# Paged attention: two pages side by side on the partitions, interlaced before, in two blocks of 64 after

## The reference, cut to what matters

```
cache_sb_kv  (1, n_pool, 128, 2, 8, 64)   float32: page, token, key or value, head, column
page_table   (8, 64)                      int32

z = q . k / 8 + bias[head]                                  for every past and new token before the query
w = sigmoid(z) * product over later tokens of sigmoid(-z)
out = sum over tokens of w * v
```

## Time and profile before

| what | value |
|---|---|
| median of three runs | 3929.19 us (3927.13 to 3931.07) |
| time of the profiled execution | 3932.51 us |
| its span in the trace | 3930.7 us |
| granted clock of TensorE, mean over the span | 0.958 of full speed |
| busy: TensorE matmul, VectorE, ScalarE, GpSimd | 91%, 48%, 30%, 20% of the span |
| read from HBM | 447.51 MB, of it 512 pages of 512 KB |

### The profile page before, as it was taken

One profiled execution on the slowest core, in us unless ns is written; L12 is line 12 of the kernel. 1 busy time (PEld: TensorE's weight loads), 2 busy tenths in 40 slices (PEclk: granted clock), 3 DMA queues, 4 the chain that ended last, 5 costly groups with the idle time before them and its releaser, 6 DMA issues. The chain is left out here.

```text
span 3930.7 us, 66394 instructions
## 1 busy us (share of the span) xinstructions
PE 3579.0 (91%) x25825; PEld 2949.1 (75%) x25825; DVE 1894.2 (48%) x2770; ACT 1166.0 (30%) x2440; POOL 770.0 (20%) x629
## 2 busy tenths in 40 slices
PE   9988888888777999999998999769987799999998
PEld 9965666666566799999997787446566699999997
DVE  2158574434376634444444366545128934444445
ACT  2156544444412121111114245321115121111112
POOL 0047122222110211111113111036111211111112
PEclk9999999999988999999999999879988899999999
DMA  3110899999703011111112201038523011111112
GB/s 134 45 51 1 337 415 415 413 413 411 307 2 122 12 44 43 43 43 47 49 43 84 70 12 33 20 126 296 172 80 107 24 44 43 43 43 43 43 43 78
DMA packets 187494, 470.75 MB, mean 120 GB/s; under 512 B 31625, under 2 KB 128773, under 8 KB 151382
## 3 DMA queue, kind: packets, MB, share of 16 engines
q1 hardware_dynamic: 166278, 446.50, 30.5%
q10 hardware_dynamic: 20976, 20.97, 1.6%
HBM read 447.51 MB, written 19.91 MB: 119 GB/s over the span
## 5 line engine op out<-in xcount | busy, mean ns | idle before, releaser
L1965 DVE TENSOR_TENSOR x<-x,f_d 128x512 f32<-128x512 f32 x540 | 368.3, 687 | 310.1 <-PE f_d L1777 249.5
L1933 POOL TENSOR_TENSOR f_hl<-f_h,f_hh 128x364 fp32r<-128x364 f32 (+1 forms) x192 | 177.5, 932 | 1267.7 <-ACT f_hh L1893 1267.7
L1982 DVE TENSOR_TENSOR f_h<-f_h 128x364 f32<-128x364 f32 (+1 forms) x192 | 103.1, 537 | 541.3 <-ACT f_h L1887 541.1
L1777 PE MATMUL f_d<-f_w2l,f_hh 128*128 128x512 f32 x896 | 354.4, 396 | 0.0
L1777 PE MATMUL f_d<-f_w2h,f_hl 128*128 128x512 f32 x896 | 354.4, 396 | 0.0
L1777 PE MATMUL f_d<-f_w2h,f_hh 128*128 128x512 f32 x896 | 354.4, 395 | 0.0
L761 DVE COPY ss_kT<-ss_tk 128x512 f32<-128x512 f32 x256 | 176.8, 692 | 327.7 <-PE ss_tk L653 212.0
L1887 ACT ACTIVATE f_h<-f_u 128x364 f32<-128x364 f32 (+1 forms) x192 | 91.2, 475 | 577.4 <-PE f_u L1777 577.4
L1777 PE MATMUL f_u<-xH,w1h 128*128 128x364 f32 (+1 forms) x768 | 254.0, 331 | 2.5 <-DVEq L1967 2.5
L1777 PE MATMUL f_u<-xL,w1h 128*128 128x364 f32 (+1 forms) x768 | 253.8, 330 | 0.0
L1777 PE MATMUL f_u<-xH,w1l 128*128 128x364 f32 (+1 forms) x768 | 253.7, 330 | 0.0
(11 more groups left out here) (588 smaller groups left out, 7893.6 us busy)
## 6 DMA issues: line engine op xcount, KB each, us to landing
ss_kv<-in_cache_sb_kv SPq DMA_DIRECT2D x336, 512.0 KB, 6.4
x<-in_cache_sb_kv SPq DMA_DIRECT2D x176, 512.0 KB, 6.2
w<-in_ffn_w SPq DMA_DIRECT2D x64, 1024.0 KB, 5.2
mp_qb<-mp_q SPq DMA_DIRECT2D x24, 1024.0 KB, 6.7
pe_raw<-in_w_in_even SPq DMA_DIRECT2D x8, 1024.0 KB, 7.1
mp_kc<-in_cache_dil_kv SPq DMA_DIRECT2D x8, 1024.0 KB, 7.7
mp_vc<-in_cache_dil_kv ACTq DMA_DIRECT2D x8, 1024.0 KB, 6.9
mp_w<-in_w_in_odd ACTq DMA_DIRECT2D x7, 1024.0 KB, 6.0
```

The lines of the kernel that those rows point to most:

```text
L1777: mm = pe.matmul(out, a, b, start=(n == 0), stop=(n == len(parts) - 1))
L1933: low = lambda dst, n0, n1, at: g.tensor_tensor(dst, h[:, u % HSLOTS, n0 - at:n1 - at], hh[:, c % 2, f, n0:n1].bitcast(F32), ALU.subtract)
L1965: v.tensor_tensor(K.x[0:r, t, cs], K.x[0:r, t, cs], dn_b[(c * DOWN + u) % 4][0:r, :], ALU.add).then_inc(added, 1)
L1982: v.tensor_tensor(x, x, x, ALU.mult).then_inc(squared, 1)
```

## The change

A page now goes to a block of 64 neighbouring partitions: the first page of a step and sequence to partitions 0 to 63, the second to 64 to 127. Before, the first went to the even and the second to the odd partitions. What runs over the partitions (after the transposes: over the columns) is therefore ordered page first and pair second, and the patterns of the two key copies, of GpSimd's product and of the weights' transposes follow. The number of DMAs, their bytes and their 8,192-byte runs, all instructions and all waits stay as they are, and so does the order of the columns of `kT`, `z` and `left`.

```diff
-                half = self.kv[g % SLOTS][pg::2, 2 * b:2 * b + 2, :]
+                half = self.kv[g % SLOTS][PAIRS * pg:PAIRS * (pg + 1), 2 * b:2 * b + 2, :]
                 sp.dma_start(half, self.cache[bass.ds(page, 1), :, :, :]).then_inc(...)
...
-        w, wT = sb("w", [P, 2, 2, PAIRS, 2]), sb("wT", [P, 2, 2 * PAGE])
+        w, wT = sb("w", [P, 2, 2, 2, PAIRS]), sb("wT", [P, 2, 2 * PAGE])
...
-   mm = pe.transpose(wb[...], w[:, g % 2, r, :, :].rearrange("p q a -> p (q a)"), K.ident[:, :])
+   mm = pe.transpose(wb[...], w[:, g % 2, r, :, :].rearrange("p a q -> p (a q)"), K.ident[:, :])
...
-   v.tensor_copy(kT[:, g % 2, :, j // 2, :, :, j % 2], turn_b[j][...].rearrange("p c (q a) -> p c a q", a=2))
+   v.tensor_copy(kT[:, g % 2, :, j // 2, :, :, j % 2], turn_b[j][...].rearrange("p c (a q) -> p c a q", a=2))
...
-   p.tensor_tensor(w[:, g % 2], z[...].rearrange("p (a q r) -> p r q a", a=2, r=2),
-                   left[...].rearrange("p (a q r) -> p r q a", a=2, r=2), ALU.mult)
+   p.tensor_tensor(w[:, g % 2], z[...].rearrange("p (a q r) -> p r a q", a=2, r=2),
+                   left[...].rearrange("p (a q r) -> p r a q", a=2, r=2), ALU.mult)
```

More of the change, by code:

```diff
@@ L674, in turn_weights @@
                     for r in range(2):
-                        mm = pe.transpose(wb[:, r * P:(r + 1) * P], w[:, g % 2, r, :, :].rearrange("p q a -> p (q a)"), K.ident[:, :])
+                        mm = pe.transpose(wb[:, r * P:(r + 1) * P], w[:, g % 2, r, :, :].rearrange("p a q -> p (a q)"), K.ident[:, :])
                     mm.then_inc(S["w_turned"], 1)
@@ L760, in copy_keys @@
                         v.wait_ge(S["logits"], g - 1)
-                    v.tensor_copy(kT[:, g % 2, :, j // 2, :, :, j % 2], turn_b[j][:, :, :].rearrange("p c (q a) -> p c a q", a=2)).then_inc(k_copied[1], 1)
+                    v.tensor_copy(kT[:, g % 2, :, j // 2, :, :, j % 2], turn_b[j][:, :, :].rearrange("p c (a q) -> p c a q", a=2)).then_inc(k_copied[1], 1)
                 copy_keys(0, 1)
@@ L828, in _ @@
                         p.wait_ge(S["w_turned"], g - 1)
-                    p.tensor_tensor(w[:, g % 2, :, :, :], z[:, g % 2, :].rearrange("p (a q r) -> p r q a", a=2, r=2),
-                                    left[:, g % 3, 1:2 * PAGE + 1].rearrange("p (a q r) -> p r q a", a=2, r=2), ALU.mult).then_inc(S["weights"], 1)
+                    p.tensor_tensor(w[:, g % 2, :, :, :], z[:, g % 2, :].rearrange("p (a q r) -> p r a q", a=2, r=2),
+                                    left[:, g % 3, 1:2 * PAGE + 1].rearrange("p (a q r) -> p r a q", a=2, r=2), ALU.mult).then_inc(S["weights"], 1)
             @block.scalar
@@ L839, in copy_keys @@
                         a.wait_ge(S["logits"], g - 1)
-                    a.activation(kT[:, g % 2, :, j // 2, :, :, j % 2], turn_b[j][:, :, :].rearrange("p c (q a) -> p c a q", a=2), ACT.Copy).then_inc(k_copied[0], 1)
+                    a.activation(kT[:, g % 2, :, j // 2, :, :, j % 2], turn_b[j][:, :, :].rearrange("p c (a q) -> p c a q", a=2), ACT.Copy).then_inc(k_copied[0], 1)
                 def shares(g):
```

## The result

| | before | after |
|---|---|---|
| median | 3929.96 us (4 runs) | 4385.82 us (4362.32 to 4388.68, 4 runs) |
| ratio of the two | | 1.114 (95%: 1.1122 to 1.1159) |
| span of the profiled execution | 3930.7 us | 4386.8 us |
| stage of the change: last matmul of line 689 begins | 1066.8 us | 1517.5 us |

The changed kernel is 11.4% slower. The forecast was 3948 us; the time lies between two of the rivals, "half way" (4117) and "half rate" (4561), and nearer to the latter. The range over all cases (3918 to 4565) holds it; that of the likeliest case (3925 to 3975), on which the forecast stood, doesn't. The instructions of the engines are the same in number and order; what changed is how long the transfers take.

What follows compares the result with a forecast made beforehand. It took page transfers at 413 GB/s to bound one stage, with SP's pace nearly equal. 3932.5 + 2.5 (restart) + 16 (stream) = 3951 us, less 3.3 us to the median: 3948 us, range 3918 to 4565, likeliest case 3925 to 3975.

Steps and rivals of the forecast that it cites:

- half way: Page stream: never leaves its state just after a start, 317 GB/s, +188 us, 4117 us; chance 0.14.
- half rate: Every page of the stage: engines stay on the same half together, 206 GB/s, +623 us, 4561 us; chance 0.30.
- the likeliest case: Transfer-bound stage: both readable collision costs doubled, 3948 us, own range 3925 to 3975; chance 0.40.
- I take it that the engines fall into step as they do now, over a longer way: Page stream: DMA engines recover after each start as before, only later; basis of +2.5 and +16 us.
- the restart: Stage at 430 to 440 us: 320 GB/s against 424 free loses 2.5 us; once more that, +2.5 us.
- the slow stretches after each start: Page stream: collisions that end some 8 us later, three times out of three; taken as evidence against half rate.
- an engine that is one page ahead works on the other half than the one it collided with: Page queue: pages alternate between lower and upper half, so a lead of one page avoids the collision.
- (b): Steady stream: 413 against 424 GB/s costs 16 us as collisions; doubled, +16 us.
- The store: A store running at 206 GB/s against 410, taken as evidence for half rate but weighed below the running stream.
- Can I just issue two DMAs to hit both halves?: Skill section: two concurrent transfers, one to each half, measured only +6% over one; implied half rate for good.
- the marks that I had named: Stage signs: at half rate 206 GB/s, some thirteen slices, TensorE at 4, landing over 20 us, SP waiting nearly every step.

Runs made afterwards that it cites:

- v4: Page stream without attention, each page to the block of partitions 32 to 95: 422 GB/s.
- v7: Page stream without attention, two pages in one DMA on 128 partitions: 422 GB/s.
- e5: The changed kernel with each page on all 128 partitions, one token of 4,096 bytes on each: 3948.25 us, 1.0043 times the kernel before.
- m1: One launch without attention: seven streams of page DMAs from SP into 12 SBUF slots, 96 pages each, differing in destination partitions; 206 to 422 GB/s.
- w1: Page stream of blocks 0 to 63 and 64 to 127 in turn, behind added DMAs of 1, 2, ... 15 runs; its set of four gave 222 to 230 GB/s.
- w4: Page stream of blocks 0 to 63 and 64 to 127 in turn, behind added DMAs of 8 runs; its set of four gave 222 to 230 GB/s.
- u8: Page stream without attention, lower-half pages from SP's queue while upper-half pages come from ScalarE's queue: 239 GB/s together.
- u9: Page stream without attention, upper-half pages from ScalarE's queue while lower-half pages come from SP's queue: 239 GB/s together.
- e6: The kernel before, with SP reading both page numbers of a sequence in one load instead of two: 3930.76 us, 0.9996 times the kernel before.
- v1: Page stream without attention, pages on every second partition: 422 GB/s.
- v3: Page stream without attention, every page to the lower block of 64 partitions: 206 GB/s.
- v2: Page stream without attention, blocks of 64 partitions, lower and upper in turn: 219 GB/s.
- y3: Page stream without attention, two DMAs of 16 rows of 16 KB, step eight from partitions 0 and 4, on eight ports each: between 205 and 241 GB/s.
- w5: Page stream of blocks of 64, lower and upper in turn, with eight pages out instead of 24: 221 GB/s.
- u1: Page stream without attention, interlaced, even and odd partitions in turn: 422 GB/s.
- u2: Page stream without attention, each page on 128 partitions in runs of 4 KB: 409 GB/s.
- y2: Page stream without attention, a page as two DMAs of 32 rows, step of four partitions, all 16 ports in each: 410 GB/s.
- u5: Stream without attention, 32 rows per DMA to partitions 0 to 31: 205 GB/s.
- u3: Page stream without attention, alternating blocks of 64 with only two pages out at a time: 145 GB/s.

## Why the prediction was wrong

What bounds the stage was read rightly: the transfers, and 1% of their rate is 6 us. So was what it says of the engines: copies, product, transposes and SP's DMA instruction (469 ns now) cost nothing.

The step that failed is "I take it that the engines fall into step as they do now, over a longer way". It gave +2.5 us for the restart and +16 us for the stream; the stream cost +434 us (255.9 MB at 243 GB/s are 1053 us, not 619.5). Two readings under it were false.

The first: I took the slow stretches after each start for collisions that dissolve, and drew from them that a collision is a matter of moments. They are no such collisions. v4 and v7 reach all ports with each DMA and have them too, as has e5 in the kernel itself (281 GB/s at share 0.83 over 430 to 440 us). What makes a start slow stays open. Of m1, the starts of v4 (first issue 602.6 us) and v7 (1188.7 us):

```profile
604.00:608.00 4.00, 0.00 (x0) 1.00 1.01 305
608.00:612.00 4.00, 0.00 (x0) 1.00 0.97 383
1190.00:1194.00 4.00, 0.00 (x0) 1.00 0.91 365
```

The second: "an engine that is one page ahead works on the other half than the one it collided with". w1 to w4 made engines go ahead and at most 5% came of it (230 against 219), and two queues (u8, u9) gave 239. In the changed kernel the rate creeps up, but never gets near 413: 215 GB/s in 430 to 440 us, 231 in 500 to 600, 262 at the most.

Both terms of the sum fall with this. For the doubling of the two costs no run shows a reason. And the 11 GB/s between 413 and 424, which term (b) priced as a collision, belong to a kernel whose DMAs all reach all ports; with a faster SP (e6) it still ran at 414, and why it stays under the 422 of v1 no run shows.

The store was the right row, 206 GB/s at share one, and v3 runs at 206. That the two agree to the number is luck: the row is half a microsecond of one store with a share read over 1. I weighed it as one store against a running stream, when it was the only row shown in which a DMA touched a block of 64, and the running stream had no row of that kind. The rule of the Trainium skill ("Can I just issue two DMAs to hit both halves?" on the page "SBUF — State Buffer") was right for the streams: they show +6% of v2 over v3, 219 against 206. The kernel got more, 243.

The rival "half rate" had the place right (every page) and that it lasts, and the size 175 us too large. Its reason, engines that stay on the same half together, is not shown: a lead didn't help, and by y3 it is the ports of a DMA that count and not the half. The term that was mis-sized is the rate, 206 for 243. In the streams a change of ports from one DMA to the next gives some time back. A page takes 524,288 B / 206 GB/s = 2.545 us in v3, 2.394 at 219 with one change (v2), 2.250 at 233 with two (v6): about 0.15 us each, an estimate from these three. That leaves the kernel open, as its pages, ordered as in v2, take 2.157 us at 243 GB/s, and its rate drifts between 231 and 262 from one stretch of 100 us to the next. A short queue is not the reason (w5, eight pages out, 221). "Half way" (4117) was priced by the state after a start, which streams on all ports have too.

Of the marks that I had named, those of half rate came, though weaker: ten slices at little over half instead of thirteen at 206 GB/s, TensorE at 6 instead of 4, SP waiting in nearly every step (122 waits), 16.1 us to landing instead of over 20. TensorE's waits grew by 308.8 us, not by the whole, since its own instructions also got longer at a clock of 0.82: its busy time per us fell only from 88% to 65%.

**Still open.** Why a DMA engine that is ahead can't use the free ports of the next DMA, although it does begin with the next one (in w1 pages moved while the added DMAs were still under way); and what lifts the kernel from 219 to 243 GB/s. The single 8 KB packets in the traces give a lead: their median is 311 ns in v4, 639 ns in v3 and 614 ns in v2, and none of v2 takes under 450 ns, but in the changed kernel (450 to 1490 us) the median is 562 ns and 11% take less than 450. So there some engines do get past the others at times. No run tests what allows it.

## What to carry to other kernels

Judge the destination of each DMA by itself: a DMA on half of the ports ran at half the rate here (206 GB/s for 422), and neither the next one in the queue, nor another queue, nor a lead made up for more than a part of it (243 GB/s in the kernel). With half of the partitions at hand, take every second one, or the block from 32 to 95 (both 422 GB/s), not the one from 0 to 63. And when one row in the trace shows exactly the operation that a change brings in, price the change by it, even where a richer row of another kind tells a kinder story.

## What the runs showed of the hardware

- Every stream of which each DMA reached all ports ran at 409 to 422 GB/s: with whole pages in 8 KB runs 422 (v1, v4, v7, u1), with 4 KB runs 409 (u2), with half pages in 8 KB runs 410 (y2). All others, with four pages or more out, ran between 205 and 241.
- 32 rows on partitions 0 to 31 (u5, 205) are as fast as 64 on 0 to 63 (v3, 206).
- The DMA share doesn't tell the two apart: 1.01 to 1.02 at 422 and at 206 GB/s. A full share with few GB/s was the mark of DMAs on half of the ports.
- With only two pages out (u3) the alternating blocks ran at 145 GB/s, share 0.63, as each pair of pages waited for the one before it to land (5.6 us after issue in the median).
- TensorE's granted clock was 1.00 in the stage before the change, with TensorE busy 88% of the time, and between 0.76 and 0.88 (means of 100 us) after it, with TensorE busy 65% of the time. That didn't set the time, as TensorE waited for pages there.
